# One-hot tiles of a transformer's expert gates, built eight tokens at a time

## What is computed

```python
def peer(h, wq, k1, k2, u, v):
    ...
    idx = jnp.take_along_axis(cand_idx, pos, axis=-1)
    g = jax.nn.softmax(sc, axis=-1).astype(t.dtype)
    def block(args):
        tb, ib, gb = args
        act = jax.nn.gelu(jnp.einsum('thkd,td->thk', u[ib], tb), approximate=False)
        return jnp.einsum('thk,thkd->td', gb * act, v[ib])
```

## Time and profile before

| | us |
|---|---|
| median of three runs | 3032.23 |
| lowest and highest | 3029.57, 3032.71 |
| the profiled execution, its own time | 3031.12 |
| its span in the trace | 3029.1 |
| PE busy in the span | 2988.2 (99%) |
| DVE busy | 2252.1 (74%) |
| ACT busy | 1394.4 (46%) |
| POOL busy | 186.1 (6%) |

### The profile page before, as it was taken

The page is one execution under the profiler, slowest core; times in us unless marked ns, Lnnn a source line. Parts: engine busy times, 40 slices in busy tenths (PEclk is TensorE's granted clock), DMA queues, the critical chain, the costliest instruction groups (busy, mean ns, idle before and its releaser), DMA issues.

```text
span 3029.1 us, 49592 instructions
## 1 busy us (share of the span) xinstructions
PE 2988.2 (99%) x19430; PEld 2798.3 (92%) x19430; DVE 2252.1 (74%) x3296; ACT 1394.4 (46%) x1494; POOL 186.1 (6%) x233
## 2 busy tenths in 40 slices
PE   8999999999999999999999999999999999999998
PEld 8899889999999999999999999999788888888887
DVE  5777559999868888888988877798656646555564
ACT  4464444466435454545454455434445333333333
POOL 1000000020001121111111000000000000000000
PEclk9999999999999999999999999999999999999999
DMA  5533454567669999999999874544444555555554
GB/s 212 179 140 140 153 201 178 191 229 254 238 251 333 342 350 363 347 354 350 354 351 352 319 273 161 193 166 166 158 174 167 185 194 193 193 185 190 194 191 156
DMA packets 102148, 705.60 MB, mean 233 GB/s; under 512 B 13016, under 2 KB 13040, under 8 KB 18464
## 3 DMA queue, kind: packets, MB, share of 16 engines
q1 hardware_dynamic: 78272, 562.07, 50.9%
q0 software_dynamic: 21872, 128.10, 12.0%
q10 hardware_dynamic: 1872, 13.63, 1.1%
HBM read 685.46 MB, written 18.24 MB: 232 GB/s over the span
## 4 chain that ended last, share of the span: by engine, by line
PE 90%; DVE 7%; ACT 1%; issue 1%; DMA 1%; POOL 0%; POOLq 0%; DVEq 0%; ACTq 0%
PE bank L2070 29%; PE bank L2057 16%; PE bank L2035 7%; PE bank L2021 7%; PE bank L2036 7%; PE bank L2114 7%; PE bank L2098 7%; PE bank L2115 7%; DVE pick_a L1633 2%; DVE split L1159 1%; DVE pick_b L1628 1%; PE bank L2183 1%; DVE raw_lo L1159 1%; ACT split L718 1%; PE bank L2147 0%
## 5 line engine op out<-in xcount | busy, mean ns | idle before, releaser
L718 ACT ACTIVATE split<-raw 128x2048 fp32r<-128x2048 f32 x532 | 1018.3, 1914 | 942.6 <-PE bank L2070 449.8
L1159 DVE TENSOR_TENSOR raw_lo<-raw,split 128x2048 fp32r<-128x2048 f32 x292 | 668.7, 2290 | 388.7 <-ACT split L718 387.5
L2070 PE MATMUL bank<-a_both,split 128*128 128x416 f32 (+1 forms) x4096 | 898.0, 364 | 4.0 <-DVE split L1159 3.8
L2070 PEld LDWEIGHTS bank<-a_both,split 128*128 128x128 f32 x4096 | 752.5, 189 | 46.5 <-issue 3.9
L1159 DVE TENSOR_TENSOR split<-raw,split 128x2048 fp32r<-128x2048 f32 x240 | 549.0, 2288 | 55.7 <-ACT split L718 35.9
L2035 PE MATMUL bank<-a_both,split 128*128 128x256 f32 (+1 forms) x1984 | 489.4, 287 | 2.1 <-DVE a_both L1178 2.1
L2036 PE MATMUL bank<-a_both,split 128*128 128x256 f32 (+1 forms) x1984 | 479.2, 281 | 0.0
L2057 PE MATMUL bank<-a_both,split 128*128 128x208 f32 x3072 | 417.7, 272 | 0.0
L2057 PEld LDWEIGHTS bank<-a_both,split 128*128 128x128 f32 x3072 | 396.3, 192 | 0.6
L2035 PEld LDWEIGHTS bank<-a_both,split 128*128 128x128 f32 x1984 | 381.8, 192 | 6.5 <-issue 2.6
L2036 PEld LDWEIGHTS bank<-a_both,split 128*128 128x128 f32 x1984 | 381.9, 193 | 0.6
(11 more groups left out here) (346 smaller groups left out, 2581.3 us busy)
## 6 DMA issues: line engine op xcount, KB each, us to landing
raw<-stream_dram SPq DMA_DIRECT2D x532, 1024.0 KB, 4.8
gates_scratch<-stage ACTq DMA_DIRECT2D x13, 1024.0 KB, 4.2
gbuf<-gates_scratch POOLq DMA_DIRECT2D x30, 416.0 KB, 7.7
x<-x_dram SPq DMA_DIRECT2D x4, 512.0 KB, 6.7
x_scratch<-x POOLq DMA_DIRECT2D x1, 2048.0 KB, 11.2
mem<-mem_dram POOLq DMA_DIRECT2D x1, 2048.0 KB, 10.0
xm<-x_scratch POOLq DMA_DIRECT2D x1, 2048.0 KB, 12.9
out_dram<-x SPq DMA_DIRECT2D x4, 512.0 KB, 3.0
```

What stands on the lines that cost most here:

```text
L718: eng.activation(high(k, is_near(k))[:, :], raw[:, k % RAW, :], ACT.Copy).then_inc(hi_done, 1)
L1159: eng.tensor_tensor(low(k, is_near(k)), raw[:, k % RAW, :], high(k, is_near(k))[:, :].bitcast(F32), ALU.subtract).then_inc(split_done, 1)
L2070: last = mm(o, hi[:, kt * P:kt * P + P], tile(kt), start=kt == 0, stop=False, skip_group_check=True)
```

## The change

The tiles are built for eight tokens at once, a pair of groups. `picks` is called for even groups only, with the number of the pair, at the place in the order where the even group stood. It has three instructions of 8 x 128 columns: compare for `pick_a`, compare for `pick_b`, and then `pick_a` times the weight, in place, behind a wait for the first. Both tiles have room for two pairs, sixteen tokens, and a pair is written over when PE has multiplied the pair two before. PE waits once for each group, for its pair's `pick_b` and for the multiplied `pick_a`. Three tables move in the work area.

```diff
-        pick_a = at("pick_a", [P, 8, P], F32, work_at + 24576)
-        pick_b = at("pick_b", [P, 8, P], F32, work_at + 28672)
+        pick_a = at("pick_a", [P, 16, P], F32, work_at + 24576)
+        pick_b = at("pick_b", [P, 16, P], F32, work_at + 32768)
...
-            def picks(q):
-
-                if q >= 2:
-                    eng.wait_ge(g_mm, 4 * (q - 1))
-                j = 4 * (q % 2)
-                eng.tensor_tensor(pick_b[:, j:j + 4, :], C("iota").unsqueeze(1).to_broadcast([P, 4, P]),
-                                  pickT[:, 1, G + 4 * q:G + 4 * q + 4].unsqueeze(2).to_broadcast([P, 4, P]),
-                                  ALU.is_equal).then_inc(ohb_done, 1)
-                for i in range(4):
-                    t = G + 4 * q + i
-                    eng.tensor_scalar(pick_a[:, j + i, :], C("iota"), pickT[:, 0, t:t + 1], pickT[:, 2, t:t + 1],
-                                      ALU.is_equal, ALU.mult).then_inc(oha_done, 1)
+            def picks(p):
+
+                if p >= 2:
+                    eng.wait_ge(g_mm, 8 * (p - 1))
+                js, ts = slice(8 * (p % 2), 8 * (p % 2) + 8), slice(G + 8 * p, G + 8 * p + 8)
+                places = C("iota").unsqueeze(1).to_broadcast([P, 8, P])
+
+                def each(n):
+                    return pickT[:, n, ts].unsqueeze(2).to_broadcast([P, 8, P])
+
+                own.did(eng.tensor_tensor(pick_a[:, js, :], places, each(0), ALU.is_equal))
+                eng.tensor_tensor(pick_b[:, js, :], places, each(1), ALU.is_equal).then_inc(ohb_done, 1)
+                own.wait()
+                eng.tensor_tensor(pick_a[:, js, :], pick_a[:, js, :], each(2), ALU.mult).then_inc(oha_done, 1)
 
             for k in range(LAST_GROUP + 1):
                 for n, q in enumerate(GATES_UNIT[k]):
                     if n == min(2, len(GATES_UNIT[k]) - 1):
                         ahead(UNIT0["u1"] + k - 1)
-                    picks(q)
+                    if q % 2 == 0:
+                        picks(q // 2)
...
             def gate_group(q):
 
-                eng.wait_ge(ohb_done, q + 1)
+                eng.wait_ge(ohb_done, q // 2 + 1)
+                eng.wait_ge(oha_done, q // 2 + 1)
                 if q >= 4:
                     eng.wait_ge(g_evict, q - 3)
                 for i in range(4):
-                    eng.wait_ge(oha_done, 4 * q + i + 1)
-                    j = 4 * (q % 2) + i
+                    j = 4 * (q % 4) + i
```

More of the change, by code:

```diff
@@ L240, in build @@
         upper = at("upper", [P, PICKS], U32, pk + 13440)
-        picked = at("picked", [P, TT, 3, PICKS], F32, pk + 6656)
-        pickT = at("pickT", [P, 3, T], F32, pk + 9728)
+        picked = at("picked", [P, TT, 3, PICKS], F32, pk + 8192)
+        pickT = at("pickT", [P, 3, T], F32, pk + 11264)
         gsum = at("gsum", [P, TT, PEER_HEADS], F32, pk + 12800)
```

## The result

The changed kernel takes 3050.93 us in the median of four runs (3049.93 to 3052.72), the kernel before 3031.57 (four runs, 3029.57 to 3032.71): a ratio of 1.0064, with a 95% interval from 1.0052 to 1.0077. It is slower by 0.64%, about 19 us, where 14 were forecast. The profiled execution took 3049.93 us with a span of 3047.9, 18.8 us more than that of the kernel before.

A forecast was written before the change was run, and what follows sets the result against it. DVE was taken to set the pace in u1, the picks stretch; DVE's extra work (6.3 us) plus waiting for ACT's copy made 14.1 us on 3031.1, so 3045.2 us. Its own range was 3043.5 to 3049, the full range 3037 to 3055.

The forecast's parts named there:

- The bound: In the picks stretch DVE sets the pace, though PE is busy 99% overall; what is lost there, the end loses.
- The price of the instructions: On DVE, three 1024-column instructions at 1.135 us make a pair 3.41 us against 3.26, 4 us in all.
- the line through 512 and 2048 columns: DVE instruction cost from two measured widths: 1.04 ns a column and 0.07 us to start, so 1.135 us for 1024.
- The estimate of 31 us of DVE work lost: From the skill's rates and fixed cost: old pair 2.20 us, new 3.38, so 1.18 us lost per pair.
- The loop: DVE's split, the pair behind it, PE's waiting group, ACT's copy, next split: two units take 22.86 us, before 20.69.
- the clock falls: Rival, 8%: PE's waits of some 2.4 us lower its clock, five times 1.7 us on top, 3054 us.
- Only DVE's work counts: Rival, 10%: ACT's copies come early enough, so only DVE's 6.3 us, or 4, are lost: 3035 to 3037.5 us.
- The number of instructions decides: Rival, 4%: a 1024-column DVE instruction costs hardly more than 0.60 us, so the kernel gets 5 us faster, 3026.
- Its upper bound: The most the picks stretch could give: 0.5 us in ten units and some 2 us of first waits, about 7 us, 3024.

The follow-up runs named there:

- late_split: The changed kernel with DVE's split of the next unit ahead of the last group's place instead of the third's; 3035.43 us, ratio 1.0012.
- old_instr_pair_wait: The changed kernel's order and buffers with the old 512- and 128-column instructions and one signal per pair; 3049.51 us, ratio 1.0066 to the kernel before.
- filled_waits: The changed kernel with 17 unused matmuls on PE ahead of each of six groups that wait for a pair; 3045.72 us, ratio 1.0048 to before.
- b1024_late_split: The kernel before with only pick_b built eight tokens at once, in sixteen-token buffers, and the split ahead of the last group; 3035.83 us, ratio 1.0017.

## Why the prediction was right, and where it was off

**The bound.** Right: u1 is a stretch where DVE and the hand-offs set the pace while the page's shares point to PE. A loss in u1 reached the end: 17.7 us of u1 are in the 18.8.

**The price of the instructions.** Right: 1.217 us each (1.21), 1.135 from start to start as the line through 512 and 2048 columns gave it, no wait at the third one. late_split measures the price of the work nearly by itself: 3.9 to 4.6 us, where 26 x 0.15 gave 4. The estimate of 31 us of DVE work lost, from two passages of the Trainium skill (VectorE: DVE Perf Modes, the perf-mode tier table and the fixed cost of the errata section), does not fit this kernel. By the same page's rule to minimize the op count (Rules for kernel authors) seven instructions fewer per pair would have come out faster, and late_split shows them 3.9 us slower.

**The loop.** Right but for one leg, which is 0.1 to 0.3 us longer than forecast: from the split's start to PE's group 5.80 (641.96 to 647.76; forecast 5.83), from the fourth group to the next split 4.67 (660.38 to 665.05; 4.7), from the third 6.82 (647.76 to 654.58) where ACT has a block of gates to send in between, and 6.62 in the next, against 6.5. At the 6.62 the copy was ready 0.2 us earlier: DVE's own two pairs end last there, which the prediction had at 6.8 and took as covered. Up to group 50 the forecast was 14.1; measured are 16.13, of which 1.6 belong to the clock (24.71 less the 23.09 from 10 to 20, where the block of gates falls in the same way), so 14.5. late_split and old_instr_pair_wait take the loop apart from both sides: the work without the coarse wait at the split costs 3.9, the coarse wait without the work about 11.5 (128.4 - 116.9).

**The clock: the term that was missing.** What the sum lacked is the rival "the clock falls". I set it as a case of 8% that happens at all five waits or at none, since the waits of the kernel before up to 1.5 us had left the clock alone and the only row with a fall had a wait of 3.8. It belonged in the sum. Waits of 2.2 us brought it down twice in six times in the changed kernel, waits of 2.05 to 2.08 five times in five in old_instr_pair_wait, and one of 1.62 once in three kernels, in filled_waits. The two falls are 1.62 + 1.59 = 3.2 of the change's 17.7 us; filled_waits gives 2.8 of them back in u1. So the time, 3050.9, lies between the forecast, 3045.2, and that rival, 3054. It is inside the range, but above the 3043.5 to 3049 that the forecast had as its own.

**The rest of the difference.** The profiled execution was 1.6 us behind already when u1 began, from places that the change doesn't touch. Runs of the kernel before differ by as much among themselves, so that part is chance.

**The other rivals.** "Only DVE's work counts" fell: DVE's splits waited for ACT as forecast, and the larger buffers did nothing. "The number of instructions decides" fell at the 1.135 us. Its upper bound was wrong besides: I let u1 give 7 us, with everything behind it shifting as a whole. That holds for a loss. For the larger gains the stretch behind has a limit of its own: b1024_late_split gained 3.2 us in u1, and DVE's wait for the gates' write took more than that. The room was to be seen before: the split of unit 12 was done some 0.8 us ahead of PE's need (it ends at 735.86 in the kernel before, and PE's low part of that unit starts at 736.68).

## What to carry to other kernels

Fewer and wider instructions are no gain as such. Count the columns they stream against the start-ups they save, and ask what the first consumer now waits for: one signal for a batch puts the batch's whole time into the next hand-off. Where engines hand work around in a circle, add up the circle as well as each engine's work; a place where one engine starts the moment another ends, on both sides, is such a circle. A wait of some 2 us on PE may cost 1.7 us more through the clock; here it paid to keep PE busy in it, and more to get rid of it.

## What was not expected of the hardware

The granted clock can fall from 2.4 to 1.2 GHz after waits as short as 1.6 to 2.2 us, and with waits of equal length it fell at some and not at others (one of three at 1.62 us, two of six at 2.2, five of five at 2.05 to 2.08). What picks them isn't shown by these runs; the four runs of old_instr_pair_wait, from 3046.1 to 3054.2 us, would fit a number that changes from execution to execution, but only one execution of each kernel was traced. Each fall in the changed kernel and in old_instr_pair_wait took 1.7 us of full-speed time; the one in filled_waits cost next to nothing, as it took up a wait for DVE that came right behind it. With extra matmuls in the waits, which compute nothing, the clock stayed up behind all six of them, and the kernel was 5 us faster.
